# A two-block network on one core: first block's layers written out, two weight chunks asked for in the set-up, the state-space output projection as three rounded products

## What is computed

```python
def first_block(x, positions, w_in, ...):
    for l in range(DEPTH):          # DEPTH = 2
        mix = hybrid_mixer(x, tabs, w_in[l], ..., w_o[l])       # u = x @ w_in[l] comes first, 3400 columns
        x = layer_norm(DEEPNORM_ALPHA * x + mix, ln1_g[l], ln1_b[l])
        moe = hier_moe(x, ..., expert_w_gate[l], expert_w_up[l], expert_w_down[l])   # 32 experts
        x = layer_norm(DEEPNORM_ALPHA * x + moe, ln2_g[l], ln2_b[l])
    return x

def ssd_mixer(...):
    ...                              # 8 groups of 4 heads, SSD_DI = 2048
        y = (y_f + y_b[:, ::-1] + xs * d_gr).reshape(b, l, SSD_DI)
        return rms_norm_2(y * jax.nn.silu(z), norm_g) @ w_out    # [256, 2048] @ [2048, 1024]
```

## Time and profile before

| | us |
|---|---|
| median of 3 runs | 2267.24 |
| lowest and highest | 2263.86, 2267.4 |
| the profiled execution | 2259.13 |
| its span | 2257.6 |

### The profile page before, as it was taken

The page is one execution under the profiler, slowest core; times in us unless marked ns, Lnnn a source line. Parts: engine busy times, 40 slices in busy tenths (PEclk is TensorE's granted clock), DMA queues, the critical chain, the costliest instruction groups (busy, mean ns, idle before and its releaser), DMA issues.

```text
span 2257.6 us, 32346 instructions
## 1 busy us (share of the span) xinstructions
PE 2023.1 (90%) x12006; PEld 1433.2 (63%) x12006; DVE 1204.8 (53%) x2143; ACT 718.2 (32%) x1303; POOL 167.7 (7%) x155
## 2 busy tenths in 40 slices
PE   6989889879898778969997999999989988998997
PEld 3776423327785323326886788888867777756896
DVE  3374411134473212137466686666666876836776
ACT  3462201014552101124324311121165446713332
POOL 2001100001002000014422100000100000000000
PEclk9999999999998999988998999999999998999999
DMA  7589699975597899852222232232222243334552
GB/s 225 174 287 345 250 408 409 369 299 175 195 362 258 334 389 403 342 203 75 75 75 75 97 127 96 91 112 75 83 87 91 95 149 108 117 112 150 202 187 96
DMA packets 151934, 440.37 MB, mean 195 GB/s; under 512 B 10368, under 2 KB 12848, under 8 KB 143456
## 3 DMA queue, kind: packets, MB, share of 16 engines
q1 hardware_dynamic: 142704, 412.72, 48.7%
q0 software_dynamic: 8352, 22.39, 3.4%
q10 hardware_dynamic: 720, 3.15, 0.3%
HBM read 534.52 MB, written 1.21 MB: 237 GB/s over the span
## 4 chain that ended last, share of the span: by engine, by line
PE 40%; DVE 7%; ACT 4%; DVEq 2%; issue 1%; DMA 1%; ACTq 0%; POOL 0%; SPq 0%; POOLq 0%
PE bank L2132 25%; PE bank L2223 11%; PE bank L2274 4%; DVE ARENA L3242 1%; ACT ARENA L2784 1%; PE bank L2137 1%; DVEq L2858 0%; ACT UT L2555 0%; ACTq L2558 0%; DMA W<-in_ffn_w 0%; DVE XA L2859 0%; ACT ARENA L2777 0%; DVE WLO L3183 0%; DVEq L2913 0%; DVE MHL L2924 0%
## 5 line engine op out<-in xcount | busy, mean ns | idle before, releaser
L2568 ACT ACTIVATE WPH<-W 128x1024 fp32r<-128x1024 f32 x128 | 135.6, 1064 | 399.2 <-PE bank L2132 198.8
L2132 PE MATMUL bank<-UH,WPH 128*128 128x512 f32 (+1 forms) x512 | 173.8, 339 | 6.0 <-DVE UL L2866 2.5
L2132 PE MATMUL bank<-UH,WPL 128*128 128x512 f32 (+1 forms) x512 | 172.3, 337 | 0.0
L2132 PE MATMUL bank<-UL,WPH 128*128 128x512 f32 (+1 forms) x512 | 172.3, 336 | 0.0
L2904 DVE TENSOR_TENSOR WPL<-W,WPH 128x1024 fp32r<-128x1024 f32 x128 | 153.5, 1220 | 17.5 <-ACT WPH L2568 17.5
L2223 PE MATMUL bank<-WPH,MHH 128*128 128x512 f32 x384 | 149.8, 390 | 0.3 <-DVE WPL L2904 0.3
L2223 PE MATMUL bank<-WPL,MHH 128*128 128x512 f32 x384 | 149.5, 389 | 0.0
L2223 PE MATMUL bank<-WPH,MHL 128*128 128x512 f32 x384 | 149.4, 389 | 0.0
L1457 DVE TENSOR_TENSOR H<-SG,bank 128x256 f32<-128x256 f32 x24 | 10.1, 421 | 239.2 <-ACT SG L1031 239.2
L2132 PE MATMUL bank<-ARENA 128*128 128x64 f32 (+4 forms) x528 | 106.9, 362 | 19.9 <-DVEq L3282 7.6
L727 PE MATMUL bank<-WC,H 128*32 128x512 f32 x768 | 93.2, 628 | 27.8 <-DMA WC<-in_expert_w_down 23.3
(11 more groups left out here) (454 smaller groups left out, 4191.4 us busy)
## 6 DMA issues: line engine op xcount, KB each, us to landing
WC<-in_expert_w_down SPq DMA_DIRECT2D x32, 2048.0 KB
W<-in_ffn_w SPq DMA_DIRECT2D x64, 1024.0 KB, 6.8
W<-in_ada_w SPq DMA_DIRECT2D x32, 1024.0 KB, 7.2
WA<-in_expert_w_gate SPq DMA_DIRECT2D x16, 2048.0 KB
WA<-in_expert_w_up SPq DMA_DIRECT2D x16, 2048.0 KB
W<-in_expert_w_gate SPq DMA_DIRECT2D x16, 2048.0 KB
W<-in_expert_w_up SPq DMA_DIRECT2D x16, 2048.0 KB
WC<-in_expert_w_down ACTq DMA_DIRECT2D x32, 1024.0 KB
```

What stands on the lines that cost most here:

```text
L2132: return nc.tensor.matmul(bank[r.bank(key)][0:rows, cols[0]:cols[1]], lhs, rhs, start=start, stop=stop)
L2568: nc.scalar.activation(piece_view(WPH, q), piece_src(i, q), ACT.Copy).then_inc(hi_done, 1)
```

## The change

- The five loops over the layers of the first block become Python loops: every list is written out twice, waits are for constants, and the fillers are gone.
- The set-up's SP list asks for chunks 0 and 1 of layer 0, and SP's list of the first block starts with chunk 2 there. The semaphores `w_in` are made outside for that.
- The output projection of the state-space mixer is made of three products of rounded parts. Its inputs are `YH` (ScalarE, rounded, `turned_out`) and `YL` (VectorE, the remainder, `turned_low`), its weights `SYH` (ScalarE, `out_weights_high`) and `WLO` (VectorE, `out_weights_low`), in 4 pieces a chunk, each with its own count. The bank of yT is freed by `turned_low`, and yT lies in bank 0 or 1 instead of 2. `YL`, `YH` and `SYH` lie in memory that the mixer's other tiles or the feed-forward's pieces use at other times; hence new waits on ScalarE, and `high_parts` for the first two pieces stands behind the last product.

```diff
-            with sp.Fori(0, DEPTH, 1) as l:
-                for n in range(MIX0):
+            for l in range(DEPTH):
+                for n in range(2 if l == 0 else 0, MIX0):
...
@@ setup, SP's list
             sp.dma_start(snake[:], io["snake"]).then_inc(loaded, 16)
+            for n in range(2):
+                for half in range(2):
+                    src = io["w_in"][0].rearrange("(k p) n -> p k n", p=P)[:, 4 * half:4 * half + 4, n * CHUNK:(n + 1) * CHUNK]
+                    sp.dma_start(W[:, n, 4 * half:4 * half + 4, :], src).then_inc(w_in[n], 16)
             sp.wait_ge(loaded, 64)
...
@@ plan_block2
-            r.plan(("yT", g - 1), 2)
+            r.plan(("yT", g - 1), g % 2 if g < SG_ - 1 else 3)
...
@@ out_part, TensorE
+            def out_part(n, c2, ts=range(2), kps=range(4)):
+                ci = SY.index((n, c2))
+                lo = WLO[:, number[("sy", n, c2)] % SLOTS]
+                for kp in kps:
+                    pe.wait_ge(conv_lo, NCONV + 4 * ci + kp + 1)
+                    pe.wait_ge(yl_rdy, 4 * c2 + kp + 1)
+                    for t in ts:
...
+                        for k in (2 * kp, 2 * kp + 1):
+                            kk = c2 * KT + k
+                            c0 = (kk // 2) * SEQ + t * P
+                            for z, (y, w) in enumerate(((YH, SYH[ci % 3]), (YH, lo), (YL, SYH[ci % 3]))):
+                                last = nc.tensor.matmul(bank[r.bank(key)][:, :], y[:, kk % 2, c0:c0 + P], w[:, k, :],
...
@@ ScalarE
+            def out_weights_high(ci):
...
+                for kp in range(4):
+                    if ci == 0 and kp == 2:
+                        r.filled(act, ("yo", SG_ - 2))
+                    nc.scalar.activation(SYH[ci % 3][:, 2 * kp:2 * kp + 2, :], W[:, n % SLOTS, 2 * kp:2 * kp + 2, :], ACT.Copy).then_inc(conv_hi, 1)
...
+            out_weights_high(1)
             turned_out(SG_ - 1)
+            out_weights_high(2)
             std(SQ_RMS, 0, 2)
-            high_parts(1, 0, PIECES)
...
+            out_weights_high(3)
+            std(SQ_LN[2], 0, 1)
+            r.filled(act, ("sy", 1, 1))
+            high_parts(1, 0, 2)
...
@@ VectorE
+            def turned_low(g):
...
+                for q in range(2):
+                    k = 2 * g + q
+                    last = nc.vector.scalar_tensor_tensor(YL[:, q, g * SEQ:(g + 1) * SEQ], bank[r.bank(key)][:, q * SEQ:(q + 1) * SEQ],
+                                                          NGC[:, k:k + 1], YH[:, q, g * SEQ:(g + 1) * SEQ].bitcast(F32), ALU.mult, ALU.subtract)
+                r.read_done(last, key)
...
                     group_finish(g - 1)
+                if g >= 2:
+                    turned_low(g - 2)
...
+            out_weights_low(0)
             group_finish(SG_ - 1)
+            turned_low(SG_ - 2)
```

More of the change, by code:

```diff
@@ L427, in _ @@
                 r.filled(sp, ("mix", 1, 1), l)
-                sp.nop(nofuse=True)
                 load(0, 0)
@@ L750, in combine @@
                     pe.drain().then_inc(combined, 1)
-            with pe.Fori(0, DEPTH, 1) as l:
+            for l in range(DEPTH):
                 for n in range(N_IN):
@@ L904, in copy_tile @@
                     copy(l, key, XT[:, 4 * h:4 * h + 4, t * P:(t + 1) * P], bank[r.bank(key)][:, :].rearrange("p (k n) -> p k n", k=4))
-            with act.Fori(0, DEPTH, 1) as l:
+            for l in range(DEPTH):
                 copy_tile(l, "xT", 0)
@@ L1230, in _ @@
             v.wait_ge(ctx_in, 16)
-            with v.Fori(0, DEPTH, 1) as l:
+            for l in range(DEPTH):
                 def low_weights(n):
@@ L1819, in block2 @@
             PHI = part[:].rearrange("p (b k n) -> p b k n", b=3, k=KT)
+        with ExitStack() as mixed:
+            SYH2 = mixed.enter_context(nc.sbuf_tensor("SYH2", [P, KT, CHUNK], F32R))
+            YL, YH = [mixed.enter_context(nc.sbuf_tensor(name, [P, 2, SG_ * SEQ], F32R)) for name in ("YL", "YH")]
+            SYH = [mixed.enter_context(nc.sbuf_tensor(f"SYH{q}", [P, KT, CHUNK], F32R)) for q in range(2)] + [SYH2]
         with ExitStack() as gla:
@@ L1944, in block2 @@
         rms_rdy = sem("b_ssd_squares")
+        yh_rdy, yl_rdy = sem("b_ssd_turned_high"), sem("b_ssd_turned_low")
+        NCONV = NX + 2 * SG_
+        SY = [(n, c2) for n in range(2) for c2 in range(2)]
         g_hi, g_lo = sem("b_gla_pieces_high"), sem("b_gla_pieces_low")
@@ L2484, in group_turns @@
                 r.fill_done(last, key)
[L2486 to L2497, removed]
+            def out_part(n, c2, ts=range(2), kps=range(4)):
[5 more added lines that the diff above has]
+                    for t in ts:
+                        key = ("sy", n, t)
+                        if c2 == 0 and kp == 0:
+                            r.claim(pe, key)
+                        for k in (2 * kp, 2 * kp + 1):
[3 more added lines that the diff above has]
+                                last = nc.tensor.matmul(bank[r.bank(key)][:, :], y[:, kk % 2, c0:c0 + P], w[:, k, :],
+                                                        start=kk == 0 and z == 0, stop=kk == 15 and z == 2, skip_group_check=True)
+                        if c2 == 1 and kp == 3:
+                            r.fill_done(last, key)
                 if c2 == 0:
@@ L2522, in _ @@
             out_part(1, 0)
-            out_part(1, 1)
+            out_part(1, 1, (0,))
+            out_part(1, 1, (1,))
             ffn(1, 2, X_LN[1])
@@ L3337, in sy_between @@
             def sy_between(n, t):
+                if n == 0 and t == 1:
+                    out_weights_low(3)
                 if n == 1 and t == 1:
```

70 lines of the change are left out of this document (32 added, 38 removed).

## The result

The changed kernel takes **2240.98 us** in the median of 4 runs (2236.3 to 2244.24), against 2267.32 us (2263.86 to 2268.14) for the kernel before: 26.3 us less, a ratio of 0.9891 with a 95% interval of 0.9879 to 0.9903. The forecast was 2256.3, its range 2248 to 2265. The sign was right, the size less than half of the truth, and the time fell out of the range.

The account below looks back on a forecast made before the run. Expert stretches were taken as bound by arriving weights, the projection by TensorE alone, the group loop by TensorE with loaded helpers. Terms -3.7 - 1.5 - 12.2 + 6.0 + 0.5 = -10.9 us gave 2256.3 us, range 2248 to 2265.

Parts of the forecast that it names:

- Early weights: Set-up: two weight chunks asked for there land earlier and move the work waiting for them forward, -3.7 us.
- rival E: Set-up: the early weights make it end 3 us later, so their gain is nothing; 2260 us, chance 0.08.
- Layers written out: First block's layer loops: 0.8 us saved at the change of layer, 0.7 for waits and fillers; -1.5 us.
- Three products: Output projection on TensorE: 64 full-precision products each become three rounded ones, -12.2 us with a shorter wait between halves.
- Helpers keep up: Output projection: ScalarE's roundings and VectorE's subtractions fit beside TensorE's products, priced at 0, ends 0 and +5 us.
- rival B: Output projection: chunks of the second column half land late and TensorE waits twice; 2261 us, chance 0.12.
- The bank wait: Group loop: score products wait for VectorE's new step to release their bank, +6.0 us, ends +2 and +9.
- Rival C: Group loop: the wait for the bank costs nothing since even and odd groups absorb it; 2251 us, chance 0.12.
- rival A: Group loop: five new waits let TensorE's clock fall from 2.4 to 1.2 GHz; 2278 us, slower, chance 0.06.
- Behind the projection: First feed-forward after the projection: weight pieces are rounded later, so VectorE's third low part starts later, +0.5 us.
- Terms 3 to 6: Mixer and projection: three-product projection -12.2, helpers 0, wait for the bank +6.0, later feed-forward rounding +0.5 us.
- rival D: Expert part: written-out code starves an engine while weights fill the DMA queues, +11 us; 2267 us, chance 0.07.

Follow-up runs that it names:

- the experiment: Kernel before with only the parts of the diff that touch the state-space mixer and its projection, loops kept: 2257.96 us, faster by 6.8 us.
- the three partial write-outs: Kernel before with the layer loop written out on TensorE alone, on VectorE and ScalarE, on SyncE and GpSimd: 2256.97, 2262.44 and 2261.69 us.
- the same written-out kernel: Kernel before with the five layer loops of the first block written out and nothing else changed: 2249.84 us, ratio 0.993.

## Why the prediction was wrong

1. **Early weights**, forecast -3.7: right in kind and about right in size. The part moved forward by 4.1 us in the pair of traces (39.19 to 35.09), but 1.0 of that comes with the written-out loops. The early weights' own share is some 3 us (38.2 to 35.0 and more), and the medians allow 2 to 7. The reading behind it held: DMA engines that moved nothing from 8 to 10 us move 377 GB/s there now. The set-up's end did not stay where it was: TensorE's first instruction starts at 10.58 to 10.95 us in the six traces with the early transfers and at 9.68 to 10.33 in the eight without. That is some 0.7 us and not 3, so rival E falls.
2. **Layers written out**, forecast -1.5 with ends -5 and 0: this step failed. It measured 14.9 us in the medians (13 to 19), 12 in the fit and some 10 in the traces. The change of layer was right (0.9 us). The rest was 0.7 us "for the waits and the fillers behind them", and that had two faults. The count stopped at one line of one queue, 132 of TensorE's 458 additions, with VectorE's and ScalarE's lists not read. And "they are hidden by matmuls" was carried from streams, where it is true, to handovers, where TensorE has nothing queued and its start is the path; TensorE waits for VectorE or ScalarE 70 times in the first 1190 us. Some ten us of the miss are here. The 0.8 us at the change of layer was the clue. Its rows also gave 0.15 us for the same pair inside a layer, and this was taken as the cost of nothing, where without the fillers it is 0.06. TensorE's additions alone are 14.7 us and its fillers 10.5, so a lower end of -5 had no ground.
3. **Three products**, forecast -12.2: -11.7 in the trace (57.4 to 45.7 us). One product takes 0.238 us on the mean of the 192, with the turns in it, where 0.227 was taken.
4. **Helpers keep up**, forecast 0: right. ScalarE took the third chunk at 2004.22, and no product waited, so rival B falls.
5. **The bank wait**, forecast +6.0 (ends +2 and +9): +5.0 (the trace of after is 12.6 us ahead at 1854 and 7.5 at 1992, the projection's start). The waits are 1.56 and 0.56 in turn instead of 1.9, all five count, and 5.8 is their sum. Rival C falls. So does rival A: the granted clock is 1.00 from 1880 to 1980 and from 1905 to 2030 in spite of the waits.
6. **Behind the projection**, forecast +0.5: 0.0. TensorE is 19.2 us ahead at 2054 and at 2240.

Terms 3 to 6 sum to 5.7 in the forecast, 6.7 in the trace and 6.8 in the experiment. Of the 15.3 us by which the median was missed, by the fit the layers have some 10.6 and the early weights some 2.6, and the last 2 lie within the scatter. The traces bear out the first but not the second of these. For rival D, code that comes late, there is a small sign: waits of TensorE for nothing but issue in the experts' products, 2.7 us in seven times in before, are 3.9 in after and, in the second trace of the changed kernel:

```profile
PE bank L673 <- issue: 6.1, 10, 2.1
```

A longest one of 2.1 us did not occur before (0.4). Such waits stand in every trace whose TensorE list is written out (0.94 us between 249 and 261 us and between 726 and 739 us in all nine, one of 1.8 to 2.1 us in six), the one with TensorE's list alone written out among them, and in none of the five with TensorE's loop. So they belong to TensorE's own list. They cost 1 to 3 us of the gain, an estimate from the growth of that line; whether it is code was not tested. By the Trainium skill, "Runtime: NRT & Kernel Launch", section "Instruction fetch mechanics", code is fetched ahead in sequence, and a taken branch whose target is outside the two-page window stalls until it has come. TensorE's written-out list has no loop branch, and these waits are in it all the same, so the rule does not explain them; for the loop's own branch no run here separates it from the computed values.

## What to carry to other kernels

A wait on a computed value costs nothing that shows in a stream, and it shows at a handover: count such instructions, and the fillers behind them, over every line of every queue, and take the full length of those at waits that end with the engine idle as the far end of the range. When a step is put behind others on a helper and releases a bank, the place of the release in that list is worth as much as the step: two 0.4 us operations cost TensorE 5 us in one place and 0.2 in another. And size a change that touches many places by medians: single traces of one kernel differed here by as much as the effect. Where traces are compared all the same, take stretches with the same time at the lower clock.

## What the hardware showed unexpectedly

Six executions of the same written-out kernel took 2245.86 to 2261.01 us. The kernel before spread as wide in one session (11 executions, 2255.85 to 2271.08) and less in another (25, 2260.18 to 2270.13). The slowest of the six had a mean granted clock of 0.954 and the others 0.961 to 0.963. In its trace TensorE stood at the lower level for 136 of the first 1192 us, and for 99 to 113 us in the six other written-out traces. Up to there these programs differ only in the time of four transfers, so such a difference can't be read as an effect of a change. The same holds on a smaller scale at the start of the state-space loop: 3.4 us more at the lower level go with 1.5 to 1.7 us more time (138.0 beside 139.6, 143.0 beside 144.7), in kernels that are the same. And the three partial write-outs summed to 12.5 us where all at once gave 12 to 15: within the intervals, shortened handovers of different engines add up.
